# Two of the last three expert pairs trade places in a streamed mixture of experts

## The reference, cut to what matters

```
g_logits = ht @ w_gr + b_gr                    # 4 groups, top 1
e_logits = per group: ht @ w_er + b_er         # 8 experts, top 2 in the group
comb     = one_hot(group) * (softmax over the top 2) * p_group
for each group:                                # weights of 8 experts at a time
    a = ht @ w_gate ; b = ht @ w_up
    out += (silu(a) * b * comb) @ w_down
x = x + out ; return rms_norm(x, g_final)
```

## Time and profile before

| | |
|---|---|
| median of 3 runs | 671.44 us |
| profiled execution | 670.38 us |
| its span, first to last instruction | 668.6 us |
| outside the span | 1.8 us |
| mean granted TensorE clock | 0.948 |
| TensorE busy (matmuls) | 582.1 us, 87% |
| bytes moved | 149.04 MB, 223 GB/s over the span |

### The profile page before, as it was taken

The page is one execution under the profiler, slowest core; times in us unless marked ns, Lnnn a source line. Parts: engine busy times, 40 slices in busy tenths (PEclk is TensorE's granted clock), DMA queues, the critical chain, the costliest instruction groups (busy, mean ns, idle before and its releaser), DMA issues.

```text
span 668.6 us, 12464 instructions
## 1 busy us (share of the span) xinstructions
PE 582.1 (87%) x4367; PEld 393.3 (59%) x4368; DVE 344.0 (51%) x853; ACT 257.7 (39%) x445; POOL 295.1 (44%) x466
## 2 busy tenths in 40 slices
PE   3899999999999999999999586889989839786992
PEld 3487788877665666877889563444444414342440
DVE  4417999999978996479042862121121101111146
ACT  6335333345665665643322104333333313333132
POOL 5343344469996222346720016454544522535230
PEclk9899999999999999999998558999999969999897
DMA  9132632622222033034089949999899999999773
GB/s 293 28 104 65 214 101 65 135 63 64 63 64 64 0 123 130 0 126 157 1 314 323 370 158 406 407 408 409 350 408 410 407 403 407 405 382 399 308 260 125
DMA packets 64606, 149.04 MB, mean 223 GB/s; under 512 B 14372, under 2 KB 30756, under 8 KB 64574
## 3 DMA queue, kind: packets, MB, share of 16 engines
q1 hardware_dynamic: 59150, 139.90, 56.5%
q0 software_dynamic: 5280, 8.22, 3.3%
q10 hardware_dynamic: 144, 0.52, 0.3%
HBM read 145.11 MB, written 12.60 MB: 236 GB/s over the span
## 4 chain that ended last, share of the span: by engine, by line
PE 49%; DVE 17%; SPq 17%; DMA 8%; issue 4%; ACT 3%; POOL 1%; POOLq 0%; DVEq 0%; ACTq 0%
PE bank L698 26%; SPq L429 12%; PE bank L1007 6%; DVE bm L1456 5%; DVE m L1455 4%; SPq L439 4%; PE bank L1024 4%; DMA region<-in_w_e_down 3%; DVE conv_buf L1447 3%; DMA gates<-in_w_e_up 2%; PE bank L776 2%; PE bank L968 2%; PE bank L809 2%; PE bank L926 1%; PE bank L797 1%
## 5 line engine op out<-in xcount | busy, mean ns | idle before, releaser
L698 PE MATMUL bank<-h_hi,w_part 128*128 128x512 f32 (+1 forms) x528 | 174.6, 400 | 3.2 <-DVE h_lo L1405 1.7
L551 POOL TENSOR_TENSOR w_part<-region,w_part 128x1024 fp32r<-128x1024 f32 (+1 forms) x52 | 109.8, 2112 | 146.8 <-ACT w_part L1094 146.8
L698 PEld LDWEIGHTS bank<-h_hi,w_part 128*128 128x128 f32 (+1 forms) x528 | 98.3, 186 | 31.1 <-issue 8.2
L1007 PE MATMUL bank<-region,kT 128*32 128x256 f32 x1536 | 91.4, 392 | 19.5 <-DMA region<-in_w_e_up 15.0
L698 PE MATMUL bank<-h_lo,w_part 128*128 128x512 f32 (+1 forms) x264 | 103.5, 392 | 0.0
L1782 DVE TENSOR_TENSOR mask_b<-mask_b,bank 128x128 f32<-128x128 f32 x30 | 8.6, 287 | 181.3 <-ACT mask_b L1356 181.3
L1007 PEld LDWEIGHTS bank<-region,kT 128*32 128x32 f32 x1536 | 54.9, 113 | 63.0 <-issue 39.3
L1094 ACT ACTIVATE w_part<-region 128x1024 fp32r<-128x1024 f32 (+1 forms) x52 | 48.0, 925 | 106.4 <-PE bank L698 106.2
L601 POOL TENSOR_TENSOR carrier<-mhalf 128x1 f32<-128x1 f32 x183 | 33.0, 198 | 121.9 <-ACT qT L1363 104.8
L1490 DVE SCALAR_TENSOR_TENSOR bank<-glu,cv,bank 128x256 f32<-128x256 f32 x196 | 78.6, 477 | 0.0
L1024 PE MATMUL bank<-region,mask_b 128*32 128x512 f32 x384 | 46.9, 606 | 12.0 <-DVE mask_b L1785 10.1
(11 more groups left out here) (285 smaller groups left out, 911.5 us busy)
## 6 DMA issues: line engine op xcount, KB each, us to landing
region<-in_w_e_down SPq DMA_DIRECT2D x22, 1024.0 KB, 16.0
region<-in_w_e_gate SPq DMA_DIRECT2D x44, 512.0 KB
region<-in_w_e_up SPq DMA_DIRECT2D x44, 512.0 KB
region<-in_w_in SPq DMA_DIRECT2D x16, 1024.0 KB, 6.1
conv_buf<-in_w_e_down SPq DMA_DIRECT2D x10, 1024.0 KB, 18.3
gates<-in_w_e_gate SPq DMA_DIRECT2D x20, 512.0 KB, 9.9
gates<-in_w_e_up SPq DMA_DIRECT2D x20, 512.0 KB, 12.5
region<-in_w_out SPq DMA_DIRECT2D x2, 2048.0 KB, 7.9
```

The costliest lines, as they stand in the source:

```text
L551: g.tensor_tensor(unit_part(u, 1), unit_raw(u), unit_part(u, 0).bitcast(F32), ALU.subtract)\
L698: last = mm(out_, a_parts[p], b_parts[q], start=start and x_ == 0, stop=stop and x_ == 2)
L1007: last = mm(bank[0][32 * c:32 * c + 32, 0:FF], xTs[:, k, at_:at_ + 32], w_gu[slot][:, e, :, half, k, j * P:(j + 1) * P], start=(half == 0 ...
```

## The change

The list gives places 3 to 15. The entries of places 13 and 14 are exchanged: before, place 13 has rank 11 and place 14 rank 4; after, place 13 has rank 4 and place 14 rank 11. Place 15 keeps the smallest.

```diff
-        place_rank = list(range(SETS)) + [SETS + r for r in (5, 0, 6, 7, 1, 8, 9, 2, 10, 3, 11, 4, 12)]
+        place_rank = list(range(SETS)) + [SETS + r for r in (5, 0, 6, 7, 1, 8, 9, 2, 10, 3, 4, 11, 12)]
```

## The result

The changed kernel takes 672.45 us (median of 20 runs, 670.78 to 675.96) against 671.14 us for the kernel before in the same series (20 runs, 668.53 to 673.54). The ratio is 1.0031 with a 95% interval of 1.0017 to 1.0046, so the exchange costs between 1.1 and 3.1 us. The profiled execution has 670.78 us with a span of 669.0 us; that of before had 670.38 and 668.6. The one lies 1.67 us under its median and the other 0.76, so the pair of profiles shows less of a difference than the runs do.

What follows compares the result with a forecast made beforehand. At the experts' end the weight stream was taken to be as late as TensorE, within about a microsecond. Terms -7.35 + 6.25 + 2.61 = +1.5 us on the 671.44 us median gave 673.0 us, range 667.5 to 677.

Steps and rivals of the forecast that it cites:

- Step 1: Weight loads: the stream keeps its times; place 15's gate and up land at 633.5, down at 639.2.
- step 4: Place 15: starts at 633.75, 1.1 us sooner, at half clock costing 2.5 us; down matmuls 1.5 us later.
- Steps 2 and 3: Places 13 and 14: second tile at 612.80, place 14 at 620.09, its down matmuls at 625.25; TensorE 7.35 us earlier.
- Step 5: Reads of expert rows: issued at about 627.7, not 635.15, but held by the backlog; gain costed at nothing.
- Step 6: Tail: TensorE's end, ScalarE's copies, GpSimd's first root and VectorE's scaling all move by +1.5 us.
- The clock that stays up: Rival at place 15: no half clock after the wait; 0.5 us gained, 670.9 us; chance 0.12.
- the tail swallows it: Rival at the tail: VectorE counts, not the root; 0 to +0.5 us, 671.7 us; chance 0.10.
- Early reads that harm: Rival: row reads share bandwidth with the last weights, which land later; 675 us, or 678.2 if half; chance 0.12.
- a lighter backlog: Rival: place 15's weights land at about 628.5 with less traffic beside them; -5 us, 666.5 us; chance 0.08.
- The sum: Whole kernel: -7.35 (place 14 earlier) + 6.25 (new wait) + 2.61 (last tile to down matmuls) = +1.5 us.

Runs made afterwards that it cites:

- e10: The changed kernel run once more, unaltered, against the kernel before: 672.24 us, ratio 1.0016.
- e4: Changed kernel with the eight reads of expert rows held until TensorE has read half the last tile's weights: 672.40 us, ratio 1.0034 to the kernel before.
- e5: Kernel before with places 13 to 15 holding ranks 11, 12, 4, so the pair of two tiles is last: 678.49 us, ratio 1.0112.
- e7: Changed kernel with GpSimd's loop shortened by one test per four tiles: 671.99 us, ratio 1.0007 to the kernel before.
- e3: Changed kernel with 11 matmuls of constants into an unused bank ahead of place 15: 670.99 us, ratio 1.0018 to the kernel before.
- e9: Kernel before with 9 matmuls of constants ahead of place 14, places 12 to 14 written out of the loop: 671.94 us, ratio 1.0011.
- e6: Kernel before with GpSimd's loop shortened by one test per four tiles: 670.28 us, ratio 0.9997.
- e8: Changed kernel with 11 matmuls of constants ahead of place 15 and GpSimd's shorter loop: 670.75 us, ratio 0.9991 to the kernel before.

## Why the prediction was right

673.0 us was forecast and 672.45 measured; +1.5 us was the shift forecast, +1.3 is the difference of the medians and +1.1 to +3.1 the interval. The mechanism was right, but two terms of the sum were off in opposite directions, so that the total comes out so near is partly luck. By its steps:

- **Step 1, the stream keeps its times.** Right in that the change didn't move it, but these times aren't fixed from one execution to the next: the last tile began at 633.79 in after and at 635.75 in e10, the same kernel. What holds is the lag behind the issue: in all nine profiles where the tile that opens place 15 waited for a load, it started 15.0 to 15.4 us after SyncE had finished issuing the last up load. In before the issue was finished at 619.31 (618.15 + 1.16), so the tile could have started at 634.35 to 634.65, and did at 634.85. The gain of start that was left was thus 0.2 to 0.5 us, not the 1.1 of step 4; this is an estimate from these lags. The profile after shows 1.06 only because its stream ran 0.7 us ahead of that of before.
- **Steps 2 and 3, places 13 and 14.** Right, 612.79 for 612.80, 620.10 for 620.09 and 625.26 for 625.25. The intervals between tiles were well read; that the moments agree too was luck, since place 13 began at 605.90 in both profiles and at 607.67 in e10.
- **Step 4, the wait and the clock.** The clock fell as forecast. The start (633.79 for 633.75) agrees by the luck told under step 1. The price was mis-sized: the forecast took 2.5 us from the two starts behind a wait and named 1.3 us, from the tile at 395.18, as the other end; the profile after has 1.87 (5.53 less 3.66). The tiles that began place 15 at half clock took 5.53 (after), 4.97 (e4), 5.49 (e5, the third order), 5.40 (e10) and, in the profile of e7, 6.56 us:

```profile
637.27 6.56 PE L1008 MATMUL bank<-region,kT 128*32 128x256 f32 x64 [5.25 <-DMA region<-in_w_e_up]
```

 A mean of 5.59, that is 1.93 us over full clock. In the profile after the down matmuls came 0.83 us later, not 1.5.
- **Step 5, the reads.** Issued at 627.61 for the 627.7 forecast. "Nothing" was 0.64 us for the first row, which is no more than the 0.7 us by which this stream ran ahead; e4 takes the early issue away and finds the same time.
- **Step 6, the tail.** GpSimd began the root 0.83 us later, with TensorE's end, but the scaling moved by only 0.43. The step had the root depend on TensorE's end alone. In four profiles (before, e3, e7, e9) the root was issued while VectorE ran its fourth L1794, and each time it ended 0.44 or 0.45 us behind that instruction; in the other eight it took 0.58 us. So in before the row that VectorE waited for until 649.96 set the scaling, and that took up the first 0.40 us of the shift.
- **The rivals.** The clock that stays up came true in none of the profiles of the unfilled order of after, the one that the tail swallows it in part (0.4 of 0.83 us). Early reads that harm, and a lighter backlog, fell: place 15's last landing was 18.7 us after its issue in before and 19.0 in after.
- **The sum.** A start gain of 0.2 to 0.5 us instead of 1.1 makes the forecast too low by 0.6 to 0.9, a mean price of 1.93 instead of 2.5 makes it too high by 0.6, and the tail takes up to 0.4. In the profiles the shift at TensorE's end is best read against the stream of the same execution:

| TensorE's end, us after the issue of the last up load was finished | |
|---|---|
| order of before | 22.5 (before), 22.1 (e6) |
| order of before, clock kept up | 22.1 (e9) |
| order of after | 24.1 (after), 23.4 (e4), 25.0 (e7), 24.0 (e10) |
| order of after, clock kept up | 22.2 (e3), 22.4 (e8) |

The means of the first and third row differ by 1.8 us, and with the clock kept up the two orders end within 0.3 us of each other. The 1.8 us less the tail's 0.4 lies within the interval of the runs. That this is the whole of the measured difference is an inference from two and four profiles, not shown.

## What to carry to other kernels

Under a stream of weights that is full, the order of the jobs can't end sooner than the last landing plus the work that stands behind it; before moving work, work out how far the end already is from that sum (here 0.2 to 0.5 us of start and 0.7 us of down weights) and expect no more. Take the landing of each load from its own issue, not from the pair before it. Count what the moved work leaves behind: a wait for DMA just ahead of the last job can start it at half clock and the end pays for it in full (1.9 us on average here), where the same wait one place earlier cost the end about 0.5 us (before against e6 and e9). To see which order is better if the stream gets faster, cut the bytes of the last job in both: here the order that lost by 0.3% wins by 0.9%.

## What the runs showed of the hardware

When the clock falls in a wait of about 3.5 us was not fixed. It stayed up through waits of 3.22 (e6), 3.51 (before) and 3.58 us (e9) and through the tile behind them. In e4 it was at half before a wait of 3.53 us was over, and in e3 it was full through the whole of a wait of 3.60 us and fell 1.4 us into the tile. The tiles of e9, e4 and e3, all at place 12:

```profile
583.82 3.66 PE L1007 MATMUL bank<-region,kT 128*32 128x256 f32 x64 [3.58 <-DMA region<-in_w_e_up]
```

```profile
583.67 6.26 PE L1009 MATMUL bank<-region,kT 128*32 128x256 f32 x64 [3.53 <-DMA region<-in_w_e_up]
```

```profile
582.62 5.35 PE L1007 MATMUL bank<-region,kT 128*32 128x256 f32 x64 [3.60 <-DMA region<-in_w_e_up]
```

In e3 the granted clock is 0.96 from 583.2 to 584.0 and 0.50 in the us behind it, with TensorE busy throughout.

And the price of a start at half clock ran from 1.3 to 2.9 us for the same 64 matmuls of place 15 behind waits of 5.2 to 7.8 us, with no relation to the wait's length: 7.83 us of wait gave 5.49 us (e5), 5.25 us gave 6.56 us (e7). A term of this kind has a range of 1.6 us in itself, more than the whole effect of this change in its profile.

GpSimd's root (a 128x1 operation) ended 0.44 or 0.45 us behind VectorE's 128x1024 L1794 in each of the four profiles in which it was issued under it, and took 0.98 to 1.54 us instead of 0.58. Whether it had been issued 0.2 (e7) or 0.75 us (before) into that instruction made no difference to where it ended.
